# The state-space mixer of a decoder trunk: next inputs injected behind the states' products, next kernel ahead of the direct part, ScalarE's order to match

## The chip, the cores and the metric

The kernel runs on one core of one Trainium2 chip. The metric is device time in microseconds (us) of one execution, 1281.95 before the change. TensorE (PE, with its weight loads PEld), VectorE (DVE), ScalarE (ACT), GpSimd (POOL) and the DMA queue of SyncE (SP) each run their own instructions in the order in which they are written, and wait for each other on semaphores only.

## The reference

Two layers of a trunk of width 1024 over 528 tokens (16 meta tokens and 512 of input). Layer 0 mixes with a diagonal state space (S5), layer 1 with differential attention; each is followed by a gated convolutional FFN. The change touches the mixer of layer 0:

```python
def s5_mixer(u, a_re, a_im, log_dt, b_re, b_im, c_re, c_im, d_skip, w_glu, b_glu):
    ...  # 64 groups of 16 channels, 64 complex states each
    bu_re = jnp.einsum('blgc,gnc->blgn', ug, bb_re)
    bu_im = jnp.einsum('blgc,gnc->blgn', ug, bb_im)
    _, _, s_re, s_im = lax.associative_scan(...)
    y = (jnp.einsum('blgn,gcn->blgc', s_re, c_re.astype(f32))
         - jnp.einsum('blgn,gcn->blgc', s_im, c_im.astype(f32)))
    y = y.reshape(bsz, L, D_MODEL) + d_skip.astype(f32) * u.astype(f32)
    z = jax.nn.gelu(y).astype(u.dtype)
    h = z @ w_glu + b_glu
    val, gate = jnp.split(h, 2, axis=-1)
    return val * jax.nn.sigmoid(gate)
```

## The kernel before

**The work.** The recurrence is cut into 66 chunks of 8 tokens. Inside a chunk the output comes from a small Toeplitz kernel (the direct part), across chunks from a scan over 66 chunk states. The channels go in eight blocks b = 0 to 7 (CT = 8) of 128 channels (8 groups). After them comes the GLU product (weight units of 8 k-steps, `glu_part(n, k0, k1)`, six matmuls to a k-step), then the rest of the trunk, which is out of the change's reach. A k-step of the GLU needs the rounded GELU output of one block, so k-steps of units 0 and 1 fill TensorE beside the last block.

**What one block needs, and the names.** PE and ACT hand PSUM banks to and fro:
- `x_transposes(b)` (L684) turns the raw inputs; ACT `turn_out` (hT, L1244) reads them out. ACT `gather` (xg, L1219) regroups them, PE `u_transposes` (L695) turns them, ACT `u_out` (U, L1228) reads them out. ACT `decay` (R, L1300) fills the scan's decays.
- POOL and DVE build the input weights F1 and F2 (`input_power`, L551); PE `input_weights` (L709, L711) turns them into banks 6 and 7; ACT `weights_out` (WBT, L1278) reads them out.
- PE `inject(b)` (L744) multiplies U by WBT into banks 2 and 3; DVE `scan(b)` (first instruction L1724) and `states(b)` (Sst, last one L1745) work there; PE `state_outputs(b)` (L764) writes the states' share of the output into banks 6 and 7. DVE then makes E of the next block (`output_product`, `output_powers`) and the rotation table of the block after it (last one L1703).
- PE `kernel_products(b)` (L728, L733) makes the Toeplitz kernel; ACT `kernel_out` (KD, L1288) copies it out; the SP queue spreads it with eight transfers (TT<-KD, L603, `toeplitz(b)`); PE `direct_outputs(b)` (L772) adds the direct part to banks 6 and 7.
- ACT `gelu(b)` (Z2, L1317) reads banks 6 and 7; PE `z_transposes` (L783); ACT `z_round` (actH, L1325); PE `z_rests` (L792, L795); ACT `z_low` (actL, L1332) give the two-part GELU output for the GLU. ACT `mirror` (T, L1307, L1308) completes a rotation table.

**Waits that matter here** (unchanged unless the diff shows them): `input_weights(b)` waits for `gelu(b-2)`, since both use banks 6 and 7; `state_outputs(b)` waits for `states(b)` and for `weights_out(b+1)`; `inject(b)` for `weights_out(b)` and `u_out(b)`; `u_transposes(b)` for the first half of `states(b-1)`; `x_transposes(b)` for `kernel_out(b-1)`; `kernel_products(b)` for E of block b; `direct_outputs(b)` for the eight TT transfers; `z_low(b)` for `z_rests(b)`; `kernel_out(b)` for the TT transfers of b-1.

**What sets the order** is the order in which each engine's loop is written. PE's body for block b was inject(b), z_transposes(b-1), input_weights(b+1), z_rests(b-1), x_transposes(b+1), u_transposes(b+1), state_outputs(b), direct_outputs(b), kernel_products(b+1). ACT's was z_round(b-1), weights_out(b+1), z_low(b-1), turn_out(b+1), u_out(b+1), gather(b+2), decay(b+1), gelu(b), kernel_out(b+1), mirror(b+2), with the splits of the first GLU weights (wH, L297) put in for b = 1, 2 and 7.

Of the kernel before, what the change touches and what calls it, by code (L numbers as in the profile page):

```python
# [33 lines left out]
CT = D // P  # L34
# [106 lines left out]
def build(nc, inp, out):  # L141
# [3 lines left out]
    with ctx:  # L145
# [302 lines left out]
        y_ps = sem("y_ps")  # L448
        gelu_set = sem("gelu_set")
# [203 lines left out]
        def _(pe):  # L653
# [113 lines left out]
            def direct_outputs(b):  # L767

                pe.wait_ge(tt_in[b % 2], (b // 2 + 1) * T * 16)
                for q in range(BQ):  # L770
                    for e in range(2):
                        mm = nc.tensor.matmul(y_at(q, e), U[:, b % 2, 2 * q + e], TT[:, b % 2, :, 2 * q + e],  # L772
                                              start=False, stop=q == BQ - 1)
                mm.then_inc(y_ps, 1)
# [55 lines left out]
            u_transposes(0)  # L830
            for b in range(CT):
                inject(b)
                if b:
                    z_transposes(b - 1)
                if b + 1 < CT:
                    input_weights(b + 1)
                    if b:
                        z_rests(b - 1)
                    x_transposes(b + 1)
                    u_transposes(b + 1)  # L840
                else:
                    glu_part(0, 0, 3)
                    z_rests(b - 1)
                    glu_part(0, 3, CT - 2)
                state_outputs(b)
                direct_outputs(b)
                if b + 1 < CT:
                    kernel_products(b + 1)

# [14 lines left out]
            def glu():  # L864

                glu_part(1, 0, 2)
                z_transposes(CT - 1)
# [322 lines left out]
        def _(act):  # L1190
# [120 lines left out]
            def gelu(b):  # L1311
                act.wait_ge(y_ps, b + 1)
                if b:
                    act.wait_ge(zr_ps, b)
                for h in range(2):
                    o = Z2[:, :, :].rearrange("k j (q e c) -> k e q j c", q=BQ, e=2)[:, h]
# [32 lines left out]
            for b in range(CT):  # L1349
                if b:  # L1350
                    z_round(b - 1)
                if b in (1, 2):
                    split_hi(act, b - 1, b - 1, 0)
                if b + 1 < CT:
                    weights_out(b + 1)
                    if b:
                        z_low(b - 1)
                    turn_out(b + 1)
                    u_out(b + 1)
                    if b + 2 < CT:  # L1360
                        gather(b + 2)
                    decay(b + 1)
                if b == CT - 1:
                    z_low(b - 1)
# [3 lines left out]
                if b + 1 < CT:  # L1368
                    kernel_out(b + 1)
                    if b + 2 < CT:  # L1370
                        mirror(b + 2)
# [601 lines left out]
        def _(pool):  # L1973
# [42 lines left out]
            pool.wait_ge(v_ps, 1)  # L2016
            input_power(V, F2b, P2, Bsw, 1).then_inc(f_set, 1)
            for b in range(2, CT):
                pool.wait_ge(v_ps, b - 1)
# [113 lines left out]
```

## Time and profile before

| | before |
|---|---|
| three runs | 1280.84 to 1281.95 us, median 1281.95 |
| the profiled execution | 1282.26 us, of which the span is 1280.1 us |
| PE / PEld busy in the span | 1250.4 / 1192.2 us (98% / 93%) |
| DVE / ACT / POOL busy | 751.4 / 571.1 / 606.4 us |
| mixer, first inject to last direct part | 33.3 to 129.2 us |

The profile is one hardware-traced execution. Its span begins with the first instruction and ends with the last. A busy PE is not PE at its peak. The prediction's sums are made against the profiled execution, which is 0.3 us above the median.

### The profile page before, as it was taken

How to read it: one execution, taken by the hardware profiler on the slowest of the kernel's cores; microseconds unless marked ns; L12 is line 12 of the kernel's file. 1: busy time of each engine (PE TensorE's matmuls, PEld its weight loads, DVE VectorE, ACT ScalarE, POOL GpSimd, SP SyncE). 2: the span in 40 equal slices, each digit the busy share in tenths (PEclk: the TensorE clock that was granted, in tenths of full speed). 3: DMA queues.
4: the chain of work that ended last, by engine and by line, in shares of the span. 5: the costliest groups of instructions: out<-in, count | busy, mean ns of one | idle time of the engine just before them, and what ended most of it. 6: DMA issues, size and time to landing. Idle time of an engine off the chain costs nothing.

```text
span 1280.1 us, 26377 instructions
## 1 busy us (share of the span) xinstructions
PE 1250.4 (98%) x10371; PEld 1192.2 (93%) x10371; DVE 751.4 (59%) x1020; ACT 571.1 (45%) x957; POOL 606.4 (47%) x363
## 2 busy tenths in 40 slices
PE   5899999999999999999999999999999999999998
PEld 5888999999999999999989889889999999998886
DVE  8997222688888883111545555543688888882002
ACT  7996543343433432222666565632343333432113
POOL 5433566444344345656655544309544344444441
PEclk9999999999999999999999999999999999999999
DMA  8333332222332233333221121103323332233231
GB/s 173 66 71 77 107 99 83 83 81 85 97 98 86 78 94 100 88 97 105 76 70 50 51 67 55 51 29 100 90 76 98 98 97 86 79 98 99 99 99 66
DMA packets 179498, 108.88 MB, mean 85 GB/s; under 512 B 7100, under 2 KB 173789, under 8 KB 179165
## 3 DMA queue, kind: packets, MB, share of 16 engines
q1 hardware_dynamic: 178997, 107.31, 29.7%
q8 instruction: 51, 0.84, 0.3%
q10 hardware_dynamic: 432, 0.59, 0.2%
q14 instruction: 18, 0.15, 0.0%
HBM read 101.59 MB, written 2.10 MB: 81 GB/s over the span
## 4 chain that ended last, share of the span: by engine, by line
PE 85%; issue 6%; POOL 4%; ACT 2%; SPq 1%; DMA 1%; DVE 1%; POOLq 0%; DVEq 0%; ACTq 0%
PE ps L314 49%; PE ps L987 11%; PE ps L937 10%; PE ps L818 7%; PE ps L1024 2%; PE ps L1094 1%; SPq L603 1%; POOL acc L2033 1%; PE ps L772 1%; PE ps L1070 1%; POOL sqt L2032 1%; DMA TT<-KD 1%; ACT xg L1219 1%; PE ps L711 1%; PE ps L1028 0%
## 5 line engine op out<-in xcount | busy, mean ns | idle before, releaser
L301 POOL TENSOR_TENSOR wL<-raw,wH 128x1024 fp32r<-128x1024 f32 x182 | 445.5, 2459 | 557.2 <-ACT wH L297 530.8
L297 ACT ACTIVATE wH<-raw 128x1024 fp32r<-128x1024 f32 x182 | 186.5, 1048 | 222.6 <-PE ps L314 78.3
L314 PE MATMUL ps<-hgH,wH 128*128 128x264 f32 (+1 forms) x1408 | 285.3, 284 | 0.0
L314 PE MATMUL ps<-hgH,wL 128*128 128x264 f32 (+1 forms) x1408 | 285.3, 284 | 0.0
L314 PE MATMUL ps<-hgL,wH 128*128 128x264 f32 (+1 forms) x1408 | 285.0, 284 | 0.0
L314 PEld LDWEIGHTS ps<-hgH,wH 128*128 128x128 f32 x1408 | 218.9, 189 | 0.1
L314 PEld LDWEIGHTS ps<-hgL,wH 128*128 128x128 f32 x1408 | 218.4, 189 | 0.0
L314 PEld LDWEIGHTS ps<-hgH,wL 128*128 128x128 f32 x1408 | 217.8, 189 | 0.0
L1406 ACT ACTIVATE cg<-cg 128x528 f32<-128x528 f32 (+1 forms) x44 | 28.2, 640 | 267.9 <-DVE cg L1811 267.9
L1805 DVE TENSOR_SCALAR cv<-u,PV 128x528 f32<-128x528 f32 (+1 forms) x44 | 111.3, 2530 | 0.0
L1811 DVE SCALAR_TENSOR_TENSOR cg<-u,PV,cg 128x528 f32<-128x528 f32 (+1 forms) x88 | 99.2, 1127 | 13.0 <-DVE cv L1805 6.7
L987 PE MATMUL ps<-hgH,wH 128*128 128x264 f32 x384 | 83.2, 298 | 0.0
L987 PE MATMUL ps<-hgH,wL 128*128 128x264 f32 x384 | 78.2, 285 | 0.0
L987 PE MATMUL ps<-hgL,wH 128*128 128x264 f32 x384 | 78.0, 284 | 0.0
L314 PE MATMUL ps<-actH,wL 128*128 128x264 f32 x352 | 71.2, 283 | 0.0
L314 PE MATMUL ps<-actH,wH 128*128 128x264 f32 x352 | 71.2, 283 | 0.0
L314 PE MATMUL ps<-actL,wH 128*128 128x264 f32 x352 | 71.1, 283 | 0.0
L1811 DVE SCALAR_TENSOR_TENSOR cv<-u,PV,cv 128x528 f32<-128x528 f32 (+1 forms) x88 | 66.3, 753 | 0.0
L1833 DVE TENSOR_TENSOR ytok<-ps,fgain 128x512 f32<-128x512 f32 x4 | 2.8, 692 | 104.7 <-ACT ysq L1425 104.7
L1469 ACT ACTIVATE Pb<-ps,tiny 128x144 f32<-128x144 f32 (+4 forms) x66 | 34.8, 532 | 63.2 <-DVE tiny L1859 63.1
L987 PEld LDWEIGHTS ps<-hgH,wH 128*128 128x128 f32 x384 | 59.3, 189 | 3.9 <-issue 3.8
L1767 DVE SCALAR_TENSOR_TENSOR hgL<-hT,PV,hgH x24 | 32.9, 1371 | 45.5 <-ACT hgH L1377 45.5
(303 smaller groups left out, 2394.7 us busy)
## 6 DMA issues: line engine op xcount, KB each, us to landing
raw<-ffn_w_up SPq DMA_DIRECT2D x88, 512.0 KB, 3.8
raw<-ffn_w_down SPq DMA_DIRECT2D x38, 512.0 KB, 3.6
raw<-attn_w_qkv SPq DMA_DIRECT2D x24, 512.0 KB, 3.7
raw<-s_w_glu SPq DMA_DIRECT2D x16, 512.0 KB, 4.2
TT<-KD SPq DMA_DIRECT2D x64, 64.0 KB, 2.4
raw<-attn_w_o SPq DMA_DIRECT2D x8, 512.0 KB, 4.2
raw<-ffn_w_down SPq DMA_DIRECT2D x8, 384.0 KB, 3.4
xb<-x SPq DMA_DIRECT2D x8, 256.0 KB
```

The costliest lines, as they stand in the source:

```text
L297: nc.scalar.activation(wH[:, slot, 0:nk], raw[:, slot % 2, 0:nk], ACT.Copy).then_inc(w_hi, 1)
L301: nc.gpsimd.tensor_tensor(wL[:, slot, 0:nk], raw[:, slot % 2, 0:nk], wH[:, slot, 0:nk].bitcast(F32), ALU.subtract).then_inc(w_lo, 1)
L314: mm = nc.tensor.matmul(ps[:, bank + b, 0:tw], w[:, slot, k0 + k, :], x[:, kt, t0:t0 + tw], start=first and k == 0 and s0, stop=last and k ...
L818: mm = nc.tensor.matmul(ps[:, bank + b, 0:tw], w[:, n % 4, k, :], x[:, k, t0:t0 + tw], start=k == 0 and s0, stop=k == 7 and s1)
L937: mm = nc.tensor.matmul(ps[:, 2 * t + c, :], x[:, kt, tok], w[:, n % 4, 4 * c:4 * c + 4], start=False, stop=last and w is ws[-1] and x is ...
L987: mm = nc.tensor.matmul(ps[:, unit_bank(n) + b, 0:tw], w[:, n % 4, k, :], x[:, k, t0:t0 + tw], start=k == 0 and s0, stop=k == 7 and s1)
L1024: return nc.tensor.matmul(ps_row[:, base[c] + a:base[c] + b], q[half[c], q0:nk], k[half[c], a:b], start=True, stop=stop)
L1406: nc.scalar.activation(cg[:, t0:], cg[:, t0:], ACT.Silu).then_inc(silu_set[l], 1)
L1469: ins = nc.scalar.activation(Pb[:, c, 0:nk], score_row(i, c), ACT.Exp, bias=mn[:, c:c + 1], scale=-1.0, accum_out=esum[:, c:c + 1])
L1767: V.scalar_tensor_tensor(hgL[:, ds(ct, 1)], hT[:, ds(ct, 1)], PV[:, ds(gain, 1)], hgH[:, ds(ct, 1)].bitcast(F32), ALU.mult, ALU.subtract). ...
L1805: ins = V.tensor_scalar(c[k][:, t0:], u[:, k, 2 + t0:2 + L], col(i, CONV_W + (3 * l + 2) * 2 * FT + k * FT + q), col(i, CONV_B + l * 2 * F ...
L1811: ins = V.scalar_tensor_tensor(c[k][:, t0:], u[:, k, t0 + j:L + j], col(i, CONV_W + (3 * l + j) * 2 * FT + k * FT + q), c[k][:, t0:], ALU. ...
```

## The change

It reorders two engines' loops and splits one semaphore. On PE, `inject(b+1)` goes directly behind `state_outputs(b)`, `kernel_products(b+1)` goes ahead of `direct_outputs(b)`, `direct_outputs` fills bank 6 and then bank 7 (with a signal after each), and `input_weights(b+1)`, `z_rests` and `x_transposes` change places. ACT's order follows, and `gelu` waits for each bank apart. Beside the last block PE does two plus two k-steps of GLU unit 0 in place of three plus three. POOL waits for other semaphores than `v_ps`.

```diff
             def direct_outputs(b):
 
                 pe.wait_ge(tt_in[b % 2], (b // 2 + 1) * T * 16)
-                for q in range(BQ):
-                    for e in range(2):
+                for e in range(2):
+                    for q in range(BQ):
                         mm = nc.tensor.matmul(y_at(q, e), U[:, b % 2, 2 * q + e], TT[:, b % 2, :, 2 * q + e],
                                               start=False, stop=q == BQ - 1)
-                mm.then_inc(y_ps, 1)
+                    mm.then_inc((y_half, y_ps)[e], 1)
...
+            inject(0)
             for b in range(CT):
-                inject(b)
-                if b:
-                    z_transposes(b - 1)
                 if b + 1 < CT:
+                    x_transposes(b + 1)
                     input_weights(b + 1)
                     if b:
-                        z_rests(b - 1)
-                    x_transposes(b + 1)
+                        z_transposes(b - 1)
                     u_transposes(b + 1)
                 else:
-                    glu_part(0, 0, 3)
+                    glu_part(0, 0, 2)
+                    z_transposes(b - 1)
+                    glu_part(0, 2, 4)
+                state_outputs(b)
+                if b + 1 < CT:
+                    inject(b + 1)
+                if b:
                     z_rests(b - 1)
-                    glu_part(0, 3, CT - 2)
-                state_outputs(b)
-                direct_outputs(b)
                 if b + 1 < CT:
                     kernel_products(b + 1)
+                direct_outputs(b)
...
             def glu():
 
+                glu_part(0, 4, CT - 2)
+                z_transposes(CT - 1)
                 glu_part(1, 0, 2)
-                z_transposes(CT - 1)
...
             def gelu(b):
-                act.wait_ge(y_ps, b + 1)
                 if b:
                     act.wait_ge(zr_ps, b)
                 for h in range(2):
+                    act.wait_ge((y_half, y_ps)[h], b + 1)
...
             for b in range(CT):
+                if b + 1 < CT:
+                    turn_out(b + 1)
+                    decay(b + 1)
+                    if b in (1, 2):
+                        split_hi(act, b - 1, b - 1, 0)
+                    weights_out(b + 1)
+                    u_out(b + 1)
                 if b:
                     z_round(b - 1)
-                if b in (1, 2):
-                    split_hi(act, b - 1, b - 1, 0)
+                if b + 2 < CT:
+                    gather(b + 2)
+                if b:
+                    z_low(b - 1)
                 if b + 1 < CT:
-                    weights_out(b + 1)
-                    if b:
-                        z_low(b - 1)
-                    turn_out(b + 1)
-                    u_out(b + 1)
-                    if b + 2 < CT:
-                        gather(b + 2)
-                    decay(b + 1)
-                if b == CT - 1:
-                    z_low(b - 1)
+                    kernel_out(b + 1)
+                else:
                     act.wait_ge(ft_ps, CT)
                     split_hi(act, 2, 2, 1)
                 gelu(b)
-                if b + 1 < CT:
-                    kernel_out(b + 1)
-                    if b + 2 < CT:
-                        mirror(b + 2)
+                if b + 2 < CT:
+                    mirror(b + 2)
...
-            pool.wait_ge(v_ps, 1)
+            pool.wait_ge(f1_set, 1)
             input_power(V, F2b, P2, Bsw, 1).then_inc(f_set, 1)
             for b in range(2, CT):
                 pool.wait_ge(v_ps, b - 1)
+                pool.wait_ge(t_set, b)
                 pool.wait_ge(ft_ps, b - 1)
...
             for n in range(2):
-                pool.wait_ge(v_ps, CT - 1 + n)
+                if n == 0:
+                    pool.wait_ge(t_set, CT)
+                else:
+                    pool.wait_ge(e_set, CT)
                 split_lo(pool, n, n)
```

On TensorE, in the middle of the mixer, before (Z_91 is the GELU output, minus_id a negated identity, TT the spread kernel). The rows run from the end of z_rests through the x and u transposes, the states' products, the direct part and the next kernel to the next inject:

```order
L795 MATMUL ps<-actH,minus_id 128x264 x2
L684 MATMUL ps<-cst,xb 128x66 x8
L695 MATMUL ps<-cst,xg 128x66 x8
L764 MATMUL ps<-E,Sst 66x128 x16
L772 MATMUL ps<-TT,U 66x128 x8
L728 MATMUL ps<-E,Bst 16x128 x16
L733 MATMUL ps<-dd,cst 16x16 x8
L744 MATMUL ps<-U,WBT 64x66 x16
L783 MATMUL ps<-cst,Z_91 128x66 x8
```

The same place in the changed kernel (its lines are numbered one higher there). Before the first row stand the sixteen input-weight instructions:

```order
L784 MATMUL ps<-cst,Z_91 128x66 x8
L696 MATMUL ps<-cst,xg 128x66 x8
L765 MATMUL ps<-E,Sst 66x128 x16
L745 MATMUL ps<-U,WBT 64x66 x16
L793 MATMUL ps<-cst,Z_91 128x66 x8
L796 MATMUL ps<-actH,minus_id 128x264 x2
L729 MATMUL ps<-E,Bst 16x128 x16
L734 MATMUL ps<-dd,cst 16x16 x8
L773 MATMUL ps<-TT,U 66x128 x8
L685 MATMUL ps<-cst,xb 128x66 x8
```

The inject (L744, now L745) moved up behind the states' products, over the direct part and the kernel; z_rests (L793, L796) now stands behind it; and the direct part is last, right ahead of the x transposes and the input weights.

On ScalarE, one block's round before, in the middle of the mixer:

```order
L1325 ACTIVATE actH<-ps 128x4x66 x2
L1278 ACTIVATE WBT<-ps 128x512 x2
L1332 ACTIVATE actL<-ps 128x4x66 x2
L1244 ACTIVATE hT<-ps 128x4x66 x2
L1228 ACTIVATE U<-ps 128x264 x2
L1219 ACTIVATE xg<-xb,ssq 66x8x16 x8
L1300 ACTIVATE R<-rho 128x8x65
L1317 ACTIVATE Z_91<-ps 66x4x8x16 x2
L1288 ACTIVATE KD<-ps 16x2x8x16 x4
L1307 ACTIVATE T_103<-T_103 128x4x33
L1308 ACTIVATE T_104<-T_104 128x4x33
```

And a block's round in the changed kernel (lines four higher):

```order
L1248 ACTIVATE hT<-ps 128x4x66 x2
L1304 ACTIVATE R<-rho 128x8x65
L1282 ACTIVATE WBT<-ps 128x512 x2
L1232 ACTIVATE U<-ps 128x264 x2
L1329 ACTIVATE actH<-ps 128x4x66 x2
L1223 ACTIVATE xg<-xb,ssq 66x8x16 x8
L1336 ACTIVATE actL<-ps 128x4x66 x2
L1292 ACTIVATE KD<-ps 16x2x8x16 x4
L1321 ACTIVATE Z_91<-ps 66x4x8x16 x2
L1311 ACTIVATE T_103<-T_103 128x4x33
L1312 ACTIVATE T_104<-T_104 128x4x33
```

The kernel copy KD moved from behind the GELU to ahead of it, the low part actL from behind WBT to right ahead of KD, and hT and R to ahead of WBT.

## Rows read from the trace of the kernel before

**Rows 1.** Windows: stretch, us, busy us per engine, granted clock, DMA
```profile
core 0: us, PE busy (x) PEld busy (x) DVE busy (x) ACT busy (x) POOL busy (x), PEclk, DMA share, GB/s
...
54.44:113.20 58.76, 56.32 (x930) 51.23 (x930) 54.44 (x106) 53.05 (x138) 19.64 (x17) 1.00 0.34 66
...
128.00:236.00 108.00, 108.00 (x896) 107.85 (x895) 25.46 (x27) 47.67 (x52) 64.71 (x35) 1.00 0.31 91
```

**Rows 2.** Waits from 33 to 135 us: us in total, times, longest
```profile
DVE rt L1724 <- PE ps L744: 6.1, 7, 2.1
...
PE ps L709 <- POOL F2b L551: 2.7, 1, 2.7
...
PE ps L772 <- DMA TT<-KD: 0.9, 3, 0.5
```

**Rows 3.** Timeline of VectorE: start us, us, form, idle before
```profile
60.52 0.70 DVE L1724 TENSOR_TENSOR rt<-T,ps 128x528 f32<-128x528 f32 x1 [0.56 <-PE ps L744]
...
72.05 0.70 DVE L1724 TENSOR_TENSOR rt<-T,ps 128x528 f32<-128x528 f32 x1 [0.33 <-PE ps L744]
```

**Rows 4.** Timeline of TensorE over one block
```profile
59.26 1.15 PE L744 MATMUL ps<-U,WBT 128*64 128x66 f32 x32
60.35 0.71 PE L783 MATMUL ps<-cst,Z 66*128 66x66 f32 x8
60.90 0.28 PE L709 MATMUL ps<-cst,F1b 128*128 128x128 f32 x1
...
66.19 1.73 PEld L764 LDWEIGHTS ps<-E,Sst 64*66 64x66 f32 x32 [0.17 <-DVE Sst L1745]
...
68.09 1.96 PE L772 MATMUL ps<-TT,U 128*66 128x128 f32 x16
...
69.99 0.66 PE L728 MATMUL ps<-E,Bst 64*16 64x128 f32 x32
...
70.79 1.15 PE L744 MATMUL ps<-U,WBT 128*64 128x66 f32 x32
```

**Rows 5.** Timeline of ScalarE over one block
```profile
63.76 1.08 ACT L1278 ACTIVATE WBT<-ps 128x512 f32<-128x512 f32 x2 [0.26 <-PE ps L711]
...
64.75 1.15 ACT L1332 ACTIVATE actL<-ps 128x264 fp32r<-128x264 f32 x2
...
65.68 1.19 ACT L1244 ACTIVATE hT<-ps 128x264 f32<-128x264 f32 x2
...
69.60 0.62 ACT L1300 ACTIVATE R<-rho 128x520 f32<-128x520 f32 x1
...
70.12 1.05 ACT L1317 ACTIVATE Z<-ps 66x512 f32<-66x512 f32 x2
...
71.08 1.52 ACT L1288 ACTIVATE KD<-ps 16x256 f32<-16x256 f32 x4
...
72.51 0.30 ACT L1307 ACTIVATE T<-T 128x132 f32<-128x132 f32 x1
```

**Rows 6.** Timeline at the start of the mixer's loop
```profile
41.23 0.20 ACT L1348 ACTIVATE tiny<-tiny 128x1 f32<-128x1 f32 x1
...
41.69 1.09 ACT L1278 ACTIVATE WBT<-ps 128x512 f32<-128x512 f32 x2 [0.25 <-PE ps L711]
...
42.91 1.97 PE L764 MATMUL ps<-E,Sst 64*66 64x128 f32 x32 [0.27 <-ACT WBT L1278]
```

**Rows 7.** Timeline around the last block, and one wait for TT
```profile
80.17 1.96 PE L772 MATMUL ps<-TT,U 128*66 128x128 f32 x16 [0.48 <-DMA TT<-KD]
...
122.11 0.66 PE L792 MATMUL ps<-cst,Z 66*128 66x66 f32 x8
...
123.29 1.27 ACT L1332 ACTIVATE actL<-ps 128x264 fp32r<-128x264 f32 x2 [2.43 <-PE ps L795]
...
127.29 1.96 PE L772 MATMUL ps<-TT,U 128*66 128x128 f32 x16
```

**Rows 8.** Chain that ended last, around the last block: start us, us
```profile
123.25 2.22 PE ps L818 x18
```

**Rows 9.** Windows: the stretch of the first input-weight transposes in the loop
```profile
37.13:40.55 3.42, 3.42 (x17) 3.42 (x18) 3.32 (x7) 3.40 (x12) 3.42 (x4) 0.52 0.56 101
```

More of the change, by code:

```diff
@@ L448, in build @@
         y_ps = sem("y_ps")
+        y_half = sem("y_half")
         gelu_set = sem("gelu_set")
```

## The prediction

> **What bounds the kernel now.** I read the windows first, to see where TensorE is the limit. Behind the mixer it is full: 108.00 us busy of 108.00 from 128 to 236 us, and so, nearly, to the end. What the mixer's end gains or loses therefore arrives at the kernel's end unchanged, if the work that is left is the same. The stretch from 54.44 to 113.20 us starts and ends with the states' products of blocks 1 and 6: five blocks in 58.76 us, 11.75 us each, in which PE is busy 56.32, DVE 54.44 and ACT 53.05 us [rows 1]. All three are over 90% busy; none has more than 1.2 us of slack in a block.
>
> The waits say what the pace hangs on: VectorE's scan waited seven times for the inject, 6.1 us in all, and the direct part three times for the transfers of the spread kernel, 0.9 us in all [rows 2]. The timelines give the old ring: scan begins 60.52, states' products 66.19, direct part 68.09, kernel 69.99, inject 70.79, and the next scan 72.05, or 11.53 us [rows 3, 4]. VectorE idled only 0.33 us ahead of that scan, so its own work is 11.20 us a block [rows 3]. A block on the transfers' wait is longer, which makes the 11.75.
>
> **The change, part by part.**
>
> *The old ring opens.* Scan to states' products takes 5.67 us, the products 1.90 (66.19 to 68.09), the inject 1.09 (59.26 to 60.35) [rows 3, 4]. With the inject right behind them the ring is 5.67 + 1.90 + 1.09, some 8.8 us with the 0.17 from the inject's end (70.79 + 1.09) to the scan at 72.05 [rows 3, 4]. It bounds nothing any more. VectorE's floor of 11.20 remains, and would give 0.55 us a block.
>
> *The wait for the spread kernel goes.* From the end of KD (71.08 + 1.52 = 72.60) to the direct part that waited for it are 7.57 us [rows 5, 7]. In the new order the direct part of b stands a whole round behind kernel b, so that this is covered in every block but the last.
>
> *A new ring closes.* `input_weights(b+2)` waits for `gelu(b)`, because of banks 6 and 7. Before, ACT did the GELU as soon as the direct part was done. Now ACT owes the low part and the kernel copy first, and the low part waits for z_rests, which stands behind the inject. Once around, from the end of one GELU to the end of the next:
> - handover to PE 0.13 (WBT ends 42.78, the states' products start 42.91) [rows 6];
> - input weights until ACT can read them 2.86 (60.90 to 63.76), weights_out 1.08, handover 0.13 [rows 4 to 6];
> - states' products 1.90, inject 1.09 [rows 4];
> - z_rests until ACT can read it 1.18 (122.11 to 123.29) [rows 7];
> - z_low 0.93 (64.75 to 65.68), kernel_out 1.43 (71.08 to 72.51), GELU 1.05 [rows 5].
>
> Sum 11.78 us. Where TensorE comes out of a wait its weight load goes ahead of its matmul by up to 0.1, which is lost once or twice, so the upper bound is 11.95; I take 11.85. What is below is the case that ACT isn't late: then TensorE's own ring counts, states 1.90, inject 1.09, z_rests about 0.9, kernel 0.80, direct 1.90, the GELU's second half 0.6, then 0.13 + 2.86 + 1.08 + 0.13, or 11.4 [rows 4 to 7]. But ACT is late by the sum. Counted from the start of z_rests, ACT ends the GELU at 1.18 + 0.93 + 1.43 + 1.05 = 4.59, where TensorE would allow 0.9 + 0.80 + 1.90 + 0.6 = 4.2. The 11.85 is thus 0.1 above the 11.75 of before. The change moves the limit from one ring to another of the same length.
>
> The split into banks and `y_half` let ACT begin the GELU 0.95 us earlier, but ACT gets there only about when the whole direct part is done: worth nothing. `x_transposes(b+1)` now waits for the kernel copy right behind the direct part; that is over before the GELU is, so it is free under it. POOL's new waits put its products where they stand now, at the scan's start, one block ahead of need: nothing.
>
> *The start.* ACT ends its table work at 41.43 and then took weights_out at once, 41.69 [rows 6]. Now turn_out (0.93, as the like read-out actL) and decay (0.52, 69.60 to 70.12) stand ahead: states' products of block 0 at 41.43 + 1.45 + 1.08 + 0.13 = 44.09, before 42.91 [rows 5, 6]. From there: inject at 45.99, kernel at 47.08, its copy from about 47.98 (kernel 0.80 and some 0.1 of drain), GELU over at 50.46, input weights, WBT and handovers 4.20, so the states' products of block 1 start at 54.66, before 54.44. The earlier inject pays back the late start, to +0.2.
>
> *Block 6.* 54.66 + 5 × 11.85 = 113.91, before 113.20: +0.7.
>
> *The last block.* Here the spread kernel isn't covered: the last kernel copy ends at 113.91 + 1.90 + 1.09 + 1.18 + 0.93 + 1.52 = 120.53, plus 7.57 is 128.1 for the last direct part, before 127.29: +0.8 [rows 7]. TensorE is there at about 127 and waits 1 us. Six k-steps of the GLU lay ahead of this point before, four do now; three take 2.22 us [rows 8], so two are 1.48 us of work left over for behind it. The z transposes and rests ahead of it are the same. 0.8 + 1.5 = +2.3 us.
>
> *Sum.* The profiled execution of 1282.26 becomes 1284.6; the median of the runs shown is 0.3 lower, so 1281.95 + 2.3 = **1284.2**. With the ring at its two ends, 11.78 and 11.95, it is 1283.9 and 1284.7; half a microsecond more either way for the transfers' landing and the start gives the likeliest case's own range, 1283.2 to 1285.4.
>
> **A rule on the clock.** After 2.7 us without work [rows 2] the granted clock was 0.52 for the stretch of 3.42 us that begins with the input weights [rows 9], that is, the lower level of 1.2 GHz. The new order leaves TensorE idle for about 1.7 us ahead of the first states' products (its input weights were done for the read-out at 41.69 [rows 6], and some 0.5 us of other transposes is left behind them; it then waits to 44.09), which no row shows to be enough. A second such stretch would double matmul time, all of it then on the path: half of 3.42, 1.7 us, and the sum would be 1285.9 rather than 1284.2. The Trainium skill, TensorE: Matmul & The Clock Gate, section "What's actually happening", has it that "the default state is throttled, and activity releases the throttle". By that rule idle time here speaks for the second stretch, and the trace agrees with it in the one place shown.
>
> **The rivals.**
> - *VectorE sets the pace* (not slower). ACT gets round sooner than the rows allow, and the ring is under 11.20. For it: the direct part and its waits are off VectorE's path for certain. Against it: the sum needs to be 0.6 us too large. Then block 6 is at 54.66 + 56.0 = 110.66 (-2.5), the last direct part too, and the left-over k-steps give back 1.5: 1281.0; if ACT's start is also less late than I have it, down to 1279. It decides below 11.4 us a block.
> - *Nothing comes of it.* TensorE's own ring of 11.4: block 6 at 111.7 (-1.5), and 1.5 lost at the last block: 1282.0.
> - *A second stretch at the lower clock* (slower). As above, 1285.9; it decides if the granted clock falls again after 40.55 us. If it falls later in the mixer too, each fall costs another 1.7.
>
> **How the numbers follow.** I give the forecast 0.52, the VectorE pace 0.24, nothing 0.12, the clock 0.12. A measurement of this kernel can tell about 0.2%, 2.6 us, from no change. The forecast's 2.3 lies just inside, so 0.29 of its 0.52 goes to "same" and 0.23 to "slower"; the clock's 0.12 is slower, nothing is same, and of the VectorE pace 0.10 is faster, 0.14 same. Faster 0.10, same 0.55, slower 0.35. The range leaves out the lower part of the VectorE case and repeated falls of the clock: 1280.0 to 1286.4.
>
> **What would show it.** Right: TensorE's input weights wait in every block for ACT's GELU (some 0.4 us), the states' products for WBT (some 0.4 us), ACT's low part for z_rests; VectorE's scan still idles some 0.7 us a block, waiting for an inject that now comes from a later block start; no wait for TT but one, about 1 us, at the last direct part; states' products of block 6 near 113.9. Wrong: states' products spaced 11.2 to 11.4 us, or the first of them earlier than 43.5, or the last direct part ahead of 127.

## The result

The changed kernel takes **1287.7 us** (median of six runs, 1286.68 to 1289.52); the kernel before took 1281.39 beside it (1280.68 to 1281.95). The ratio is 1.0045, 95% interval 1.0034 to 1.0055: slower by some 6 us, where 1284.2 and a range to 1286.4 were forecast. The profiled execution of the changed kernel took 1287.97 us (span 1285.9), 5.71 us over the one of before.

Windows of the changed kernel: from the states' products of block 1 to those of block 6, from there to the last direct part, the stretch of low clock at the start, and a second one late in the kernel. They answer to [rows 1, 9].

```profile
core 0: us, PE busy (x) PEld busy (x) DVE busy (x) ACT busy (x) POOL busy (x), PEclk, DMA share, GB/s
54.65:115.09 60.44, 56.80 (x931) 50.78 (x931) 56.17 (x108) 52.46 (x137) 19.59 (x17) 1.00 0.33 65
115.09:129.81 14.72, 13.61 (x212) 11.87 (x212) 5.97 (x11) 7.19 (x17) 2.36 (x1) 1.00 0.39 83
...
36.30:43.10 6.80, 5.93 (x31) 5.93 (x32) 6.63 (x11) 6.49 (x19) 5.27 (x5) 0.50 0.52 107
...
862.30:869.10 6.80, 6.80 (x32) 6.80 (x33) 0.90 (x2) 2.15 (x3) 1.02 (x1) 0.50 0.01 2
```

Five blocks take 60.44 us, 12.09 each, in place of 58.76. At both low stretches the granted clock is 0.50, TensorE's lower level of 1.2 GHz. Each lasts 6.8 us here; in the profile of before each lasted 3.4. Its late one, around 860 us, lies in this window of the kernel before (a mean clock of 0.83 over 10 us is 3.4 us at 0.50):

```profile
858.00:868.00 10.00, 10.00 (x72) 10.00 (x72) 4.26 (x5) 3.48 (x4) 5.57 (x4) 0.83 0.19 54
```

The waits of the changed kernel from 33 to 135 us (in total, times, longest), to be read against [rows 2]:

```profile
ACT actL L1336 <- PE ps L796: 8.9, 7, 3.3
...
DVE rt L1727 <- PE ps L745: 5.3, 4, 2.7
...
PE ps L710 <- ACT Z L1321: 2.8, 6, 0.5
PE ps L765 <- ACT WBT L1282: 2.1, 7, 0.5
...
PE ps L773 <- DMA TT<-KD: 1.0, 1, 1.0
```

Most of these are the waits that the prediction named: the input weights wait for the GELU in all six later blocks, 0.5 us each, the states' products for WBT, the low part for z_rests, and TT is waited for once, 1.0 us. The waits of three direct parts for TT are gone. VectorE's scan waits longer than forecast, 0.8 to 0.9 us a block in the middle and not 0.7, as the ring is longer.

Where the 5.71 us lie, from milestones of the two profiles (the first L314 product behind the GLU starts at 219.36 and 223.32; the last row counts to the device time, about 2 us behind the span's end):

| stretch | before | after | change | forecast |
|---|---|---|---|---|
| to the first inject | 33.29 | 32.72 | -0.57 | 0 |
| to the states' products of block 1 | 21.15 | 21.93 | +0.78 | +0.22 |
| five blocks | 58.76 | 60.44 | +1.68 | +0.49 |
| to the last direct part | 14.09 | 14.72 | +0.63 | +0.10 |
| to the end of the GLU product | 92.07 | 93.51 | +1.44 | +1.48 |
| the rest of the kernel | 1062.90 | 1064.65 | +1.75 | 0 |

So 4.53 us are lost in the mixer and its GLU, and 1.75 in code that the change doesn't touch. The late low stretch begins at products of 16 columns or right behind them; half of the 3.4 us that the stretch is longer is 1.7. The traces below bear this out in kind. From the first L314 product to the span's end it is 1060.3 to 1061.0 us in the seven profiles with a late stretch of 3.4 us and 1061.4 to 1062.6 in the nine with 6.8, with either order of the mixer in both groups. The longer stretch is worth 1.1 us on average; this pair, with 1.75, is at the wide end.

### The profile page after: what moved, and what is told of

The parts are those of the page before. It is cut to its first block, busy times and chain, and to the rows that moved or that the text cites. A ratio compares the mean times of both kernels' runs of the same rounds, so it can differ in the third digit from the quotient of the medians.

```text
span 1285.9 us, 26377 instructions
## 1 busy us (share of the span) xinstructions
PE 1253.7 (97%) x10371; PEld 1194.1 (93%) x10371; DVE 751.8 (58%) x1020; ACT 570.4 (44%) x957; POOL 606.4 (47%) x363
## 4 chain that ended last, share of the span: by engine, by line
PE 86%; issue 6%; POOL 4%; ACT 2%; DVE 1%; SPq 0%; DMA 0%; POOLq 0%; DVEq 0%
PE ps L314 49%; PE ps L991 10%; PE ps L941 10%; PE ps L819 7%; PE ps L1028 2%; PE ps L1098 1%; PE ps L712 1%; PE ps L765 1%; POOL acc L2040 1%; PE ps L1074 1%; POOL sqt L2039 1%; PE ps L710 1%; ACT KD L1292 1%; PE ps L745 1%; ACT Z L1321 1%
## 5 line engine op out<-in xcount | busy, mean ns | idle before, releaser
L314 PE MATMUL ps<-hgH,wH 128*128 128x264 f32 (+1 forms) x1408 | 285.3, 284 | 0.0
L314 PE MATMUL ps<-hgH,wL 128*128 128x264 f32 (+1 forms) x1408 | 285.3, 284 | 0.0
L314 PE MATMUL ps<-hgL,wH 128*128 128x264 f32 (+1 forms) x1408 | 285.0, 284 | 0.0
L314 PEld LDWEIGHTS ps<-hgH,wH 128*128 128x128 f32 x1408 | 218.9, 189 | 0.1
L314 PEld LDWEIGHTS ps<-hgL,wH 128*128 128x128 f32 x1408 | 218.4, 189 | 0.0
L314 PEld LDWEIGHTS ps<-hgH,wL 128*128 128x128 f32 x1408 | 217.8, 189 | 0.0
L314 PE MATMUL ps<-actH,wL 128*128 128x264 f32 x352 | 71.2, 283 | 0.0
L314 PE MATMUL ps<-actH,wH 128*128 128x264 f32 x352 | 71.2, 283 | 0.0
L314 PE MATMUL ps<-actL,wH 128*128 128x264 f32 x352 | 71.2, 283 | 0.0
```

What stands on the lines that cost most here:

```text
L314: mm = nc.tensor.matmul(ps[:, bank + b, 0:tw], w[:, slot, k0 + k, :], x[:, kt, t0:t0 + tw], start=first and k == 0 and s0, stop=last and k ...
```

## The ring, term by term

ScalarE of the changed kernel, one block:

```profile
95.12 1.14 ACT L1336 ACTIVATE actL<-ps 128x264 fp32r<-128x264 f32 x2 [0.57 <-PE ps L796]
96.06 1.58 ACT L1292 ACTIVATE KD<-ps 16x256 f32<-16x256 f32 x4
97.66 1.08 ACT L1321 ACTIVATE Z<-ps 66x512 f32<-66x512 f32 x2
...
101.77 1.09 ACT L1282 ACTIVATE WBT<-ps 128x512 f32<-128x512 f32 x2 [1.16 <-PE ps L712]
```

TensorE beside it:

```profile
90.91 1.97 PE L765 MATMUL ps<-E,Sst 64*66 64x128 f32 x32 [0.27 <-ACT WBT L1282]
92.81 1.15 PE L745 MATMUL ps<-U,WBT 128*64 128x66 f32 x32
93.89 0.71 PE L793 MATMUL ps<-cst,Z 66*128 66x66 f32 x8
...
98.89 0.30 PE L710 MATMUL ps<-cst,F1a 128*128 128x128 f32 x1 [0.46 <-ACT Z L1321]
...
103.00 1.20 PE L765 MATMUL ps<-E,Sst 64*66 64x128 f32 x18 [0.27 <-ACT WBT L1282]
```

Round the ring: states' products 1.90, inject 1.08, z_rests to low part 1.23, low part 0.94, kernel copy 1.60, GELU 1.08, handover 0.15, input weights 2.88, WBT with its handover 1.23: 12.09. The forecast had 1.90, 1.09, 1.18, 0.93, 1.43, 1.05, 0.13, 2.86, 1.21: 11.78, taken as 11.85. It is the right ring; 0.17 of what is missing is the kernel copy. Its 1.43 was the distance to the table's half that followed it [rows 5], which began before the copy's end. The GELU begins only behind that end, at 97.66 (0.11 of the 0.17), and the first of the four copies took 0.41 us, where none had taken over 0.38. In r2 below, where the low part doesn't stand right ahead of the copy, the first one took 0.37 and the distance to the GELU is 1.56.

## The experiments

Medians are those of the runs of each kernel; ratios are to the kernel before, run on the same chip beside it. The labels r1 to r18 are those of the runs.

**The two kernels again** (r1, r5). No edit.

> The changed kernel itself, once more, as the measure for the other three of this call and as a second sample of the granted clock. Theory (ring): states' products 12.1 us apart again, the scan's start to block 6 unchanged, +4.5 us against before at the end of the GLU, whatever the clock does. Rival (clock): the fall of the clock at the 16-column products, which lasted 3.4 us before and 6.8 us after, is chance; then it comes out shorter or longer here, and the time moves by 1.7 us with it, 1286 or 1288.

> The kernel before, once more, for a second sample of its granted clock. In its first profile the clock fell once for 3.4 us at 37 us and once for 3.4 us at 860 us; in the changed kernel both stretches were 6.8 us, in two profiles of two. If the length of the late stretch is chance, it comes out as 3.4 or 6.8 here as well; if it belongs to the change, it is 3.4 again.

The changed kernel: 1287.26 us, ratio 1.0035 (1.0023 to 1.0048), again 12.09 us a block and two stretches of 6.83 us. The kernel before: 1282.03, ratio 1.0003 (0.9993 to 1.0013), 11.60 a block. But this profile of the kernel before has long stretches too:

```profile
35.80:42.60 6.80, 5.80 (x30) 5.81 (x31) 6.63 (x12) 5.34 (x17) 5.21 (x5) 0.50 0.39 70
858.40:865.20 6.80, 6.80 (x33) 6.80 (x33) 2.12 (x2) 2.75 (x3) 2.25 (x1) 0.50 0.01 2
```

So the order of the mixer doesn't fix the length of a stretch: one kernel shows either. But the long ones are commoner with the changed order. Of the ten profiles of the changed kernel and its variants eight have the long stretch at the start, of the ten of the kernel before and its variants two. The mean granted clock of single runs says the same: it is 0.995 or less in 11 of 12 runs of the changed kernel, and in 32 of the 98 runs of the kernel before that stood beside the experiments. Those 32 are 1.7 us slower on average than the other 66. So a part of the 6 us is clock that comes with the change; what makes the long ones commoner isn't shown. At the start the longer stretch cost r5 1.2 us at the states' products of block 1 (22.32 behind the first inject, not 21.15), of which 0.3 is left at the end of the GLU.

**ScalarE's place for the low part.** The low part behind the GELU (r2, shown), and (r3) the kernel copy behind the GELU, as before, with the x transposes behind the input weights and hT behind WBT.

```diff
-                if b:
+                if b == CT - 1:
                     z_low(b - 1)
                 if b + 1 < CT:
                     kernel_out(b + 1)
...
                 gelu(b)
+                if b and b + 1 < CT:
+                    z_low(b - 1)
```

> The changed kernel with ScalarE's low part behind the GELU instead of ahead of the kernel copy (blocks 1 to 6). Theory: the ring through z_rests, low part, kernel copy and GELU opens, but the kernel copy still stands ahead of the GELU and can't start before the kernel products, so the ring is only some 0.2 us shorter: states' products 11.9 apart, total 1 us below the changed kernel. Rival A (the low part is the whole trouble): 11.4 apart, 3.5 to 4 us below. Rival B (TensorE's own order is the limit): no change at 12.1.

> The changed kernel with the GELU ahead of the kernel copy on ScalarE, and the x transposes back behind the input weights on TensorE; inject, kernel and bank-by-bank direct part stay where the change put them. Theory: the GELU ends right behind the direct part, the ring is TensorE's own: states' products 11.7 to 11.8 apart, so about 2 us below the changed kernel, and no more, because TensorE now has nothing to do while the GELU's second half runs (0.8 us). Rival (clock and start alone made it slow): within 0.5 us of the changed kernel.

Measured 11.96 us a block and 1287.69 us (1.0044, 1.0027 to 1.0062), and 11.92 a block and 1287.61 (1.0039, 1.0025 to 1.0053). Either order shortens the ring by less than 0.2 us: moving one read-out of ScalarE doesn't open it. Neither total went down, where 1 and 2 us were expected. In r2 the first of the five blocks takes 12.56 us, so that the five together are 60.40 us, as good as the 60.44 of the changed kernel, and the last block takes 11.06, not 10.6. In r3 the first takes 12.06, and the last block loses all: its states' products come 14.4 us behind those of block 6, with a low stretch of 3.41 us there.

**The start** (r4). WBT and U of block 1 ahead of hT and R:

```diff
                 if b + 1 < CT:
-                    turn_out(b + 1)
-                    decay(b + 1)
+                    if b:
+                        turn_out(b + 1)
+                        decay(b + 1)
...
                     weights_out(b + 1)
                     u_out(b + 1)
+                    if b == 0:
+                        turn_out(b + 1)
+                        decay(b + 1)
```

> The changed kernel with turn_out and decay behind weights_out and u_out in the first round of ScalarE only. Theory (ScalarE's serial work sets the first states' products): they start up to 1.2 us earlier, 0.7 or more of it arrives at block 6 and at the end. Rival (the low clock sets them, since TensorE's input weights only end at 42.5): 0.4 us earlier or less, total within 0.4 us of the changed kernel.

1284.89 us, 1.0020 (1.0010 to 1.0029). Block 1 is at 20.77 us behind the first inject, not 21.93, and the gain is still there at the end. This profile had the short stretches (3.41 us), and nine of the ten runs a mean clock of 0.996 or more, which is part of it, as r11 and r17 show.

**The last block.** All six k-steps ahead of the last direct part (r8); then this and the mended start together (r11).

```diff
+                else:
+                    glu_part(0, 4, CT - 2)
                 direct_outputs(b)
...
-                glu_part(0, 4, CT - 2)
-                z_transposes(CT - 1)
                 glu_part(1, 0, 2)
+                z_transposes(CT - 1)
```

> The changed kernel with two more k-steps of the GLU ahead of the last direct part, six in all as before the change. Theory: the last direct part waits 1 us for its transfers, the 1.5 us of k-steps fill that and push it back by 0.5, so 1.0 us is won at the end of the GLU. Rival (these transfers land later as TensorE's work moves, or the wait reappears behind it at the z transposes): nothing is won.

> The changed kernel with both single repairs, weights_out first in the first round and six k-steps ahead of the last direct part. Theory (the parts add up: start 1.2, last block 1.0, five blocks 0.3 each over the kernel before): 2.2 to 2.5 us below the changed kernel and 1.5 to 2.5 above the kernel before at the end of the GLU. Rival (the start's gain is eaten by the wait for the last transfers): only one of the two is seen.

The first: 1286.71 us (1.0046, 1.0029 to 1.0063); the end of the GLU comes 1.1 us sooner behind the first inject (189.47, not 190.60), as expected (1.48 of k-steps that no longer stand behind it, less what they push back the direct part). Both together: 1285.69 (1.0024, 1.0014 to 1.0034). Here the start gained nothing. ScalarE of this kernel:

```profile
42.48 1.08 ACT L1283 ACTIVATE WBT<-ps 128x512 f32<-128x512 f32 x2 [1.83 <-PE ps L712]
```

It was free at 40.65 and waited 1.83 us for input weights that TensorE, at 1.2 GHz until 42.5, hadn't done. With the short stretch the same instruction started at 41.58 (r4). With the short stretch and the change's own order (r17) block 1 is at 21.56 us behind the first inject. So the mended order is worth 0.8 us with the short stretch (20.77 against 21.56) and nothing with the long one (22.12 against 21.93); the rest of the 1.2 us above is the stretch.

**Bank by bank alone** (r10), in the kernel before (the diff of `direct_outputs` and `gelu` shown above).

> The kernel before with the direct part bank by bank and the GELU waiting for each bank, alone. Theory: the GELU, and so the kernel copy and its transfers, come 0.5 us earlier; the 0.2 to 0.5 us that the direct part waited for them in every second block goes: 11.55 apart in place of 11.75, about 1 us won. Rival: the ring of scan, products and inject doesn't see it, or the kernel copy waits anyway for its products: nothing.

1282.40 us, ratio 0.9997 (0.9987 to 1.0006); 11.54 us a block. The kernel before shows 11.75 and 11.60 in its two profiles and, where only products behind the mixer were moved (r6, r18 below), 11.72 and 11.54, with unlike waits for TT, so the profile can't tell this gain from none either.

**The inject alone** (r9), in the kernel before, nothing else moved:

```diff
+            inject(0)
             for b in range(CT):
-                inject(b)
...
                 state_outputs(b)
+                if b + 1 < CT:
+                    inject(b + 1)
                 direct_outputs(b)
```

> The kernel before with one part of the change alone: the inject directly behind the states' products; kernel products behind the direct part and ScalarE's order as before. Theory: the scan is freed here too, but the inject is gone from behind the kernel products, where it hid the GELU, so that the z transposes now wait for the GELU (some 0.5 us a block), and the wait for the spread kernel stays; states' products about 11.7 apart, total within 1 us of the kernel before. Rival (the inject's place is what costs in the changed kernel): 12 us apart and 2 us or more above.

**1296.24 us**, ratio 1.0106 (1.0089 to 1.0123), far over both prices. Blocks come 13 to 14.6 us apart. VectorE of this kernel, end of E and start of the rotation table:

```profile
87.69 1.11 DVE L1696 TENSOR_TENSOR T<-TAB 128x160 f32<-128x160 f32 x1
88.73 1.23 DVE L1697 TENSOR_TENSOR tmpE<-TAB 128x160 f32<-128x160 f32 x1
89.88 1.22 DVE L1698 TENSOR_TENSOR T<-TAB 128x160 f32<-128x160 f32 x1
```

GpSimd of the same kernel:

```profile
87.13 2.65 POOL L551 TENSOR_TENSOR F1a<-P,Bst 128x512 f32<-128x512 f32 x2 [6.88 <-PE ps L744]
89.73 1.18 POOL L551 TENSOR_TENSOR F2a<-P,Bsw 128x512 f32<-128x512 f32 x1
```

The early inject releases GpSimd early (`v_ps`), and its products stand beside VectorE's table. A table row of 0.32 us then takes 1.1 to 1.2, about as long as one of GpSimd's products. In the kernel before the table was over when GpSimd began:

```profile
69.97 0.33 DVE L1694 TENSOR_TENSOR T<-TAB 128x160 f32<-128x160 f32 x1
72.04 2.18 POOL L551 TENSOR_TENSOR F1b<-P,Bst 128x512 f32<-128x512 f32 x2 [7.21 <-PE ps L744]
```

The scan's first row, with one input in PSUM (L1726 here), takes 0.70 us in all eight blocks of this kernel, four of them beside a product of GpSimd, and in the kernel before it does so beside that same product of 72.04 [rows 3]. The Trainium skill, SBUF — State Buffer, section "Who interferes with whom", says that a VectorE instruction with two SBUF inputs contends with a GpSimd instruction that reads SBUF, and that one with at most one SBUF input, outside the modes that use both port pairs, doesn't. The trace agrees on both, 0.32 to 1.11 and more, and 0.70 unchanged.

**GpSimd's waits.** Into that kernel, the change's waits for the table and E (r13); then, the other way round, the changed kernel with these undone (r14):

```diff
-            pool.wait_ge(v_ps, 1)
+            pool.wait_ge(f1_set, 1)
...
                 pool.wait_ge(v_ps, b - 1)
+                pool.wait_ge(t_set, b)
```

> The kernel before with the inject moved up (13.6 us behind before when alone) and with GpSimd's changed waits, which start input_power behind VectorE's rotation table instead of beside it. Contention theory: the table rows (128x160) take 0.32 us again instead of 1.1 to 1.2, the states' products come some 11.7 us apart, and the total is within 1.5 us of the kernel before. Rival (the moved inject itself, ahead of the direct part, is what costs): still 13 us or more apart and some 1293 to 1296 us.

> The changed kernel with GpSimd waiting for v_ps alone, as before. Contention theory: table rows above 1 us, states' products some 13.5 us apart, 1295 to 1300 us. Rival (ScalarE's ring of 12.09 hides it, or the inject's place behind a longer ring frees GpSimd late enough): states' products stay 12.1 apart and the total within 1 us of the changed kernel, 1287.

The first: 1285.65 us (1.0026, 1.0016 to 1.0035), 11.82 us a block, and VectorE's table is back at its length:

```profile
80.41 0.33 DVE L1696 TENSOR_TENSOR T<-TAB 128x160 f32<-128x160 f32 x1
80.65 0.32 DVE L1697 TENSOR_TENSOR tmpE<-TAB 128x160 f32<-128x160 f32 x1
80.89 0.32 DVE L1698 TENSOR_TENSOR T<-TAB 128x160 f32<-128x160 f32 x1
```

The second: **1294.48 us** (1.0092, 1.0075 to 1.0109), 14 us a block; groups of VectorE's instructions by line in it, ns min/median/max:

```profile
L1697 DVE TENSOR_TENSOR T<-TAB x4: 324/720/1228, 57.4 to 99.7; 128x160 f32<-128x160 f32 x4
L1699 DVE TENSOR_TENSOR T<-TAB x4: 317/1219/1225, 59.7 to 101.1; 128x160 f32<-128x160 f32 x4
```

So the line "POOL waits for other semaphores", costed at nothing, is worth 7 us in the changed kernel and 11 in the one with the inject alone. It brings no gain; it keeps the moved inject from setting two engines beside each other. Not all of the 7 and 11 is the slower rows. Inside the mixer the clock fell twice in r14 and three times in r9, for 3.41 us each, after stretches in which TensorE had waited (it was busy for 1.8 of the 3.4 us ahead of the first fall in r9); half of that, at most 3.4 and 5.1 us, is clock. The first run missed its 1.5 us. The five blocks are right; the last block isn't, 15.46 us from block 6's states' products to block 7's, where 12.20 stood. The last inject is out before the other work there, so states are ready early, but TensorE still had its k-steps and z_rests ahead of their products, idled 1.9 us in small waits and ran 3.41 us at the low clock.

**The parts together** (r16): inject, bank by bank and GpSimd's waits in the order of before.

> The kernel before with the inject moved up, the direct part bank by bank and GpSimd's changed waits, in the order of before otherwise. If the gains of the parts add: 11.5 us apart or less, total 1281 to 1282.5, with VectorE's own 11.2 as the floor. Rival: the inject ahead of the direct part delays the GELU by its 1.09 us on the ring that bounds, 11.7 to 12.0 apart, 1283 to 1285.

1283.95 us, 1.0015 (1.0005 to 1.0024); blocks 11.59 apart, the last one 14.07. The blocks are near the sum of the parts, the total is the rival's, and the last block is where it goes. A second way to shorten the wait for TT was to issue four of the eight transfers from GpSimd, with inject and banks moved and GpSimd's waits as in r9 (r12):

```diff
-                for i in range(T):
+                for i in range(T // 2):
                     sp.dma_start(TT[i * GC:(i + 1) * GC, b % 2], Kp[:, i:i + T]).then_inc(tt_in[b % 2], 16)
...
+                for i in range(T // 2, T):
+                    pool.dma_start(TT[i * GC:(i + 1) * GC, b % 2], Kp[:, i:i + T]).then_inc(tt_in2[b % 2], 16)
```

> The kernel before with the inject directly behind the states' products, the direct part bank by bank, and four of the eight transfers of each spread kernel issued from GpSimd instead of SyncE. Theory (the transfers' 7.6 us, mostly issue, are what holds the old order back once the scan is free): they land 2 us earlier, no wait for TT is left, states' products 11.3 to 11.4 apart, 1.5 to 2 us below the kernel before. Rival (GpSimd's issues are slow, or its input weights come late behind them): TensorE waits for POOL instead, same or slower.

1305.44 us, 1.0177 (1.0160 to 1.0194). TensorE waited 13.6 us for VectorE's states, and the clock fell four times in the mixer. VectorE of this kernel:

```profile
69.40 5.69 DVE L1651 TENSOR_TENSOR E<-FP,Q 128x512 f32<-128x512 f32 x2
```

And GpSimd:

```profile
70.24 2.19 POOL L553 TENSOR_TENSOR F1a<-P,Bst 128x512 f32<-128x512 f32 x2
72.38 2.16 POOL L553 TENSOR_TENSOR F2a<-P,Bsw 128x512 f32<-128x512 f32 x2
```

Two rows that take 1.29 us elsewhere end 0.5 us behind GpSimd's second product. Here GpSimd's products kept their 1.1 us each and VectorE stood; above both took turns. What decides between the two wasn't tried. As r9's old waits are in this kernel too, it doesn't tell what two queues would be worth without them.

**The late low stretch.** It begins in the attention's output product, whose 36 products of 16 columns (the meta tokens) come in two runs of 18. TensorE there in the changed kernel, first one product each 0.11 us, then one each 0.21:

```profile
862.04 0.26 PE L1141 MATMUL ps<-oH,wL 128*128 128x16 f32 x1
862.16 0.26 PE L1141 MATMUL ps<-oH,wH 128*128 128x16 f32 x1
862.27 0.35 PE L1141 MATMUL ps<-oL,wH 128*128 128x16 f32 x1
862.47 0.36 PE L1141 MATMUL ps<-oH,wL 128*128 128x16 f32 x1
862.68 0.36 PE L1141 MATMUL ps<-oH,wH 128*128 128x16 f32 x1
```

TensorE didn't idle ahead of it; the window before the fall, columns as above:

```profile
858.90:862.30 3.40, 3.40 (x33) 3.40 (x31) 0.00 (x0) 0.00 (x0) 0.00 (x0) 1.00 0.00 0
```

First they were spread so that 24 still stood in a row, in the kernel before (r6) and in the changed one (r7):

```diff
                 for n in range(2):
                     wo_products(n, (last - 1,), ALL)
-                    wo_products(n, range(last - 1), ((0, META),))
+                for i in range(3):
+                    if i < 2:
+                        wo_products(2, (5 + i,), ALL)
+                    for n in range(2):
+                        wo_products(n, range(2 * i, 2 * i + 2), ((0, META),))
```

> The kernel before with the 16-column products of the output projection (36 in a row, where the granted clock falls) spread in three parts between 264-column ones; the same instructions, the mixer untouched. Theory: the late fall goes, and with it 1.7 us of every run that had one stretch and 3.4 of those that had two. Rival: the fall has another cause, and the time is the same within 0.5 us.

> The changed kernel with the same spreading. Theory (of the 5.8 us between the two profiles 1.7 are a longer late stretch at the lower clock, the rest is the mixer): about 3.4 us below the changed kernel, and 4.0 to 4.5 us above the kernel before with the same spreading, which is what the mixer alone costs. Rival (all of it is mixer): 5.8 above it.

1282.81 us (1.0002, 0.9990 to 1.0013) and 1286.73 (1.0046, 1.0029 to 1.0063): the stretch stayed, of 3.41 and 6.83 us, and the totals with it. Then in sixes, in three kernels (r15, r18, r17), each between steps with wide products:

```diff
-                wo_products(2, range(5, last), ALL)
-                for n in range(2):
-                    wo_products(n, (last - 1,), ALL)
-                    wo_products(n, range(last - 1), ((0, META),))
+                wo_products(0, (last - 1,), ALL)
+                wo_products(0, range(0, 2), ((0, META),))
+                wo_products(1, (last - 1,), ALL)
+                wo_products(0, range(2, 4), ((0, META),))
+                wo_products(2, (5,), ALL)
+                wo_products(0, range(4, 6), ((0, META),))
...
```

> The kernel before with the direct part bank by bank, and the 16-column wo products in sixes between wide steps. If the granted clock falls at 860 us because narrow products stand in a row, the late stretch is gone: 1.7 us less than bank by bank alone had with a 3.41 us one, 3.4 less than with 6.83, so 1279 to 1281. Rival (the fall hangs on what stands ahead of the narrow products, or there are too many of them in any order): a low stretch of 3.41 or 6.83 us stays near 858 us, and the total is 1282 to 1283.

> The kernel before with the same spread and nothing else. If the late stretch is all of the gain, the same as with the split direct part beside it, 1279.9 within 0.4 us. If the direct part bank by bank has the 0.7 us that its profile showed at the GLU's end, 1280.6.

> The changed kernel with the 16-column wo products in sixes between wide steps. The late low-clock stretch was 6.83 us in both profiles of the changed kernel. If it goes as it did in the kernel before, 3.4 us less: some 1284 us, with the runs closer together than the 3 us of before; the 12.09 us ring and the GLU's end 190.5 us behind the first inject stay. Rival (the fall comes back, or comes elsewhere): 1286 to 1288.

The stretch is gone in all three, where 16 of the 17 profiles with longer rows of narrow products have one (r12 has none). Windows of the kernel with bank by bank over the place:

```profile
853.60:857.00 3.40, 3.40 (x32) 3.40 (x30) 0.12 (x1) 0.00 (x0) 0.00 (x0) 1.00 0.00 0
857.00:863.80 6.80, 6.80 (x59) 6.80 (x59) 3.45 (x3) 2.88 (x4) 4.03 (x3) 1.00 0.06 15
```

| narrow products in sixes | us | ratio, 95% |
|---|---|---|
| kernel before, nothing else (r18) | 1280.59 | 0.9989 (0.9979 to 0.9998) |
| kernel before, with bank by bank (r15) | **1279.93** | 0.9986 (0.9976 to 0.9995) |
| changed kernel (r17) | 1284.11 | 1.0020 (1.0010 to 1.0029) |

The kernel of r15 beats both, by 2.1 us over the kernel before. The intervals don't tell it from r18, so bank by bank isn't shown to have a share. With the stretch out of both, the change costs 1284.11 - 1280.59 = 3.5 us: this is the mixer's order. The clock is out of it as far as the runs tell, with means of 0.996 to 0.998 in both, and behind the GLU the two profiles agree (1058.85 and 1059.16 us to the span's end). By these profiles, each the fastest of its ten runs, the order costs more, 4.6 us up to the end of the GLU, so 3.5 is good to about 1 us.

## Why the prediction was wrong

Two steps failed: the term "kernel_out 1.43" of the ring, which is 1.60, and the step that carries the mixer's end unchanged to the kernel's end, where 1.75 us came on top. Part by part:

- *What bounds the kernel* held for the mixer: what its end lost arrived in full. But the step "arrives at the kernel's end unchanged, if the work that is left is the same" fails as a statement on time: the same work took 1.75 us more, with a second stretch at 1.2 GHz, 860 us in, that was longer. The profile of before showed that stretch; I read the clock only at the start [rows 9]. Without it (r17, r18) 3.5 of the 6.3 us between the medians are left; the spread takes 3.6 us off the changed kernel (other chips) and 1.3 off the kernel before beside it.
- *A new ring closes*: right, and shown wait by wait. The term "kernel_out 1.43" was mis-sized, 1.60; with 0.05 in z_rests and 0.02 to 0.04 each in the GELU, the input weights with their handover, and WBT it makes 12.09, beyond the upper bound of 11.95. The weight-load allowance of "up to 0.1, once or twice" is not what the gap is: the loads go ahead by 0.03 us in these blocks. Five blocks, 1.2 us.
- *VectorE sets the pace*, *nothing comes of it*: neither came, for the same reason.
- *The start*: states' products of block 0 were forecast 10.80 us behind the first inject; with the short stretch (r17) they came at 10.73, with the long one at 11.10. The first step holds; the long stretch added 0.4.
- *A second stretch at the lower clock*, given 0.12, is what happened: 6.83 us in both profiles of the changed kernel. Its reason fell: the kernel before, without the new idle time, showed the same (r5), and in the changed kernel TensorE waited 0.48 us ahead of the first states' products, not 1.7, because the longer low stretch filled the time. Its price of "all of it then on the path", 1.7, was too high: 0.4 here, because ScalarE's read-outs cover part, but 1.35 once they are moved out of the way (22.12 in r11 against 20.77 in r4). No rival had the fall behind the mixer, where most of the clock's cost was.
- *The last block*: the direct part started 8.01 us behind the end of the copy (121.80), not 7.57; one of the eight issues of the queue took 1.85 us. In r17 the same distance was 7.34, so this term moves by 0.7 us from profile to profile, and a miss of 0.4 in it is no fault of the working. The wait of 1.0 us and the two k-steps left over, 1.44 for 1.48, were right.
- *POOL's new waits: nothing.* Right as a sum, but not as a reading: without them it is 7 us more. The claim "where they stand now" held them fixed and so never asked what the moved inject would do without them.
- *How the numbers follow*: my own range of 1283.2 to 1285.4 took its width from ring and transfers alone. Through the clock, profiles with the same work can differ by 1.1 us late on average, up to 2.3, and by 0.4 early, which the range left out; and a forecast 0.3 us inside the bound between "same" and "slower" deserved more on "slower".

Against the profile the forecast missed 3.4 us: 1.2 in the ring's five blocks, 0.5 in the last block, 0.6 at the start (0.4 of it the long stretch) and 1.75 late, less 0.6 ahead of the first inject, where nothing was forecast.

What stays open: why the long stretches are commoner with the changed mixer than in the kernel before, and why the GELU's rows don't begin under the copy's end, as the table's do.

## What to carry to other kernels

Price a term of a ring by the distance from start to start only if the instruction behind it is the same in the new order; otherwise take the whole duration. When an inject, a load or any releasing step moves up, list which engines it releases, and what they then run beside: here a freed GpSimd more than tripled VectorE's table rows, and two waits were worth more than the reordering (7 us against 3.5). And read the granted clock over the whole span: the only measured gain here came from a place some 730 us behind the change.

## What the hardware showed unexpectedly

- VectorE's 128x160 rows with both inputs in SBUF: 0.32 us alone, 1.1 to 1.2 beside one of GpSimd's products (r9, r14); in r12 two 128x512 rows 5.69 us for 1.29. Rows with an input in PSUM kept their 0.70 us beside the same products.
- Products of 16 columns, one behind the other without a wait, were followed by a fall of the granted clock from 1.00 to 0.50, to the level of 1.2 GHz, though TensorE was recorded busy for the whole 3.40 us ahead of it. With six of them at a time between wider ones it stayed at 1.00. The Trainium skill, TensorE: Matmul & The Clock Gate, section "What's actually happening", has it that activity releases the throttle. Whether that agrees the rows don't settle: the clock fell with 3.40 of 3.40 us recorded busy, and the ends of matmuls are modelled in the profile.
- Low stretches were 3.41 or 6.83 us. In the four profiles of the two kernels the early and the late one had the same length each time, and so in 15 of all 16 profiles that have a late one (r14 had 6.83 and 3.41).
